# The wait for a scatter's landing in a mixture-of-experts kernel on one Trainium2 core: the copy of the scatter's targets is put ahead of it

## The chip, the cores and the metric

The kernel runs on one core of a Trainium2 chip. A core has four compute engines (TensorE, VectorE, ScalarE, GpSimd), a queue engine SyncE (SP) that mostly issues DMAs, and 16 DMA engines. The metric is the device time of one execution in microseconds, the median of several runs. Each engine runs its own instruction stream in order; the streams meet only at semaphores.

## The reference, cut to what matters

The layer has two halves. The first is attention: adaLN modulation, one combined input projection, differential attention beside grouped-query attention, an output projection and a residual. The second is a mixture of experts over 1024 tokens of width 1024. It is the second that the change touches:

```
s = sigmoid(h @ w_router)                      # 64 experts
idx, w = group-limited top 8 of 64, normalised # for each token
routed[token] += w * ((silu(h @ w_eg[e]) * (h @ w_eu[e])) @ w_ed[e])   # for its 8 experts e
x = x + gate * rmsnorm(routed + shared_expert(h))
```

Every token goes to 8 of 64 experts, so there are 8192 pairs of token and expert. An expert has a gate and an up matrix of 1024 x 256 and a down matrix of 256 x 1024, all float32.

## The kernel before

The program runs phase after phase: `front`, `attention`, `output_and_router` (which also runs the shared expert and writes its result to `y_d` in device memory), `routing_tables`, `experts`, `final`. The change lies in `experts` (from L1610).

**Blocks.** The pairs are sorted by expert and cut into blocks of 128 slots; the last block of an expert is padded. In this data that makes 104 blocks; an expert has one or two of them, seldom more. `routing_tables` makes a table with the expert, the first slot and the weight-ring place of each block. For each block n: 128 token rows of `h2_d` are gathered by index, transposed, multiplied with the expert's gate and up weights, passed through silu, scaled, transposed, multiplied with the down weights, and the 128 result rows are added to their tokens' rows in `y_d` by a scatter that accumulates.

**Precision.** Products are made from a high and a low part of both factors, three matmuls for one. ScalarE makes the high parts (`w_gate_up_high` L1747, `w_down_high` L1771) and VectorE the low parts (`w_gate_up_low` L1802, `w_down_low` L1831), for every block again.

**Who does what, in one turn n.** The four loops are written by hand and run the same number of turns, with different parts of the pipeline in one turn:

- SyncE loads each expert's weights into a ring of 5 places, when the last block that used the place has passed TensorE's down product (semaphore `dn`).
- TensorE: gate and up product of block n+1, transposes of n+2 (L1865), down product of n (`ps_ye`, L1893), transpose of the activation of n+1.
- ScalarE: high part of the activation of n, `w_down_high` of n, `w_gate_up_high` of n+2, silu of n+1, transposed rows of n+2, and then the result of n out of PSUM into one of two buffers `e_y`, in two halves (L1782 and L1784). Ahead of the first half it waits on `scat` for 16n + 16, which is the landing of the scatter of n-2, since that one read the same buffer.
- VectorE: the low parts in the same order, and `e_weight` and the gate.
- GpSimd: gathers the rows of block n+4 (a copy of 128 indices, L1692, then the indirect DMA, L1695), loads the indices of n+6 (L1683), and then scatters the result of n (a copy of the 128 target rows, L1704, then the indirect DMA, L1709).

**The scatters are kept one behind another.** A token's rows appear in blocks of several experts, and each scatter reads, adds and writes rows of `y_d`. So scatter n is not issued before scatter n-1 has landed: GpSimd waits on `scat` for 16n + 32 (the count starts at 32, from two writes of zeros). The target rows of block n come out of a ring of 8 columns (`ir`) into one of two small buffers (`si`). `carry` is a semaphore that nobody waits for.

**Order of time.** ScalarE's result of block n+1 waits for the landing of scatter n-1, and so does GpSimd's turn n. In the trace the two stand beside each other.

Of the kernel before, what the change touches and what calls it, by code (L numbers as in the profile page):

```python
# [1609 lines left out]
def experts(b, a, ident, tab, wgu, wdn, s_w, s_slots, h2_d, y_d, slot_d):  # L1610
# [3 lines left out]
    nc = b.nc  # L1614
    NS = SPLIT // 2
    RING = 8
    with ExitStack() as ph:
# [14 lines left out]
        ir = b.sb(ph, "e_index_ring", [P, RING], U32)  # L1632
        zero = b.sb(ph, "e_zero", [P, D])
        gi = [b.sb(ph, f"e_gather_index{u}", [P, 1], U32) for u in range(2)]
        si = [b.sb(ph, f"e_target_index{u}", [P, 1], U32) for u in range(2)]
# [4 lines left out]
        S = {n: b.sem(ph, "e_" + n) for n in (  # L1640
            "xT", "xH", "xL", "wH", "wL", "wused", "gu", "silu", "act", "aTp", "aH", "dh", "dl",
            "dn", "y", "weight", "rows", "target", "scat", "landed", "carry", "zeroed")}
# [4 lines left out]
        def read(eng, c, at, hi):  # L1647
            return eng.value_load(tab[0:1, c, ds(at, 1)], min_val=0, max_val=hi)

        def blocks(eng, body):  # L1650

            turns = eng.value_load(tab[0:1, 3, E:E + 1], min_val=1, max_val=NBLK // 2)
            with eng.Fori(0, turns) as i:
                for u in range(2):
                    body(i, i * 2 + u, u)
            return turns

        @block.sync
        def _(sp):

            def landed(n):
                sp.wait_ge(s_w[n % WS], (n // WS + 1) * 48)
                sp.sem_inc(S["landed"], 1)

            landed(0)
            sp.wait_ge(s_gather[1], 16)
            for n in range(PRE, WS):
                load_expert(sp, a, wgu, wdn, s_w, n)
                landed(n - 1)
            for n in range(WS, E):  # L1670
                done = read(sp, 3, n - WS, NBLK)
                sp.wait_ge(S["dn"], done * 2 + 1)
                load_expert(sp, a, wgu, wdn, s_w, n)
                landed(n - 1)
            landed(E - 1)

        @block.gpsimd
        def _(pool):
            def index(n, u):

                row = read(pool, 1, n, E * SEQ)
                pool.sem_inc(S["carry"], 1)
                pool.dma_start(ir[:, ds(n & (RING - 1), 1)], slot_d[ds(row, P), :]).then_inc(s_index[u], 16)  # L1683

            def gather(n, turn, u, first=False):

                pool.wait_ge(s_index[u], turn * 16 + 16)
                if not first:
                    pool.wait_ge(S["xT"], n * 2 - 2)
                    pool.wait_ge(S["weight"], n - 1)  # L1690
                pool.sem_inc(S["carry"], 1)
                nc.gpsimd.tensor_copy(gi[u][:], ir[:, ds(n & (RING - 1), 1)]).then_inc(S["rows"], 1)  # L1692
                pool.wait_ge(S["rows"], n + 1)
                pool.sem_inc(S["carry"], 1)
                pool.indirect_dma_start(xg[u][:], None, h2_d, bass.IndirectOffsetOnAxis(ap=gi[u][:, 0:1], axis=0),  # L1695
                                        bounds_check=SEQ - 1, oob_is_err=False).then_inc(s_gather[u], 16)

            def body(i, n, u):
                gather(n + 4, i + 2, u)
                index(n + 6, u)  # L1700

                pool.wait_ge(S["scat"], n * 16 + 32)
                pool.sem_inc(S["carry"], 1)
                nc.gpsimd.tensor_copy(si[u][:], ir[:, ds(n & (RING - 1), 1)]).then_inc(S["target"], 1)  # L1704

                pool.wait_ge(S["y"], n * 2 + 4)
                pool.wait_ge(S["target"], n + 1)
                pool.sem_inc(S["carry"], 1)
                pool.indirect_dma_start(y_d, bass.IndirectOffsetOnAxis(ap=si[u][:, 0:1], axis=0), yb[u][:], None,  # L1709
                                        bounds_check=SEQ + P - 1, compute_op=ALU.add).then_inc(S["scat"], 16)  # L1710


            for u in range(2):
                pool.wait_ge(s_slots[u], NT // 2 * TOPK * 16)
            index(0, 0)
            index(1, 1)
            for what in (xg[0], xg[1], zero):
                nc.gpsimd.memset(what[:], 0.0).then_inc(S["zeroed"], 1)
            pool.wait_ge(S["zeroed"], 3)
            gather(0, 0, 0, True)  # L1720
            gather(1, 0, 1, True)
            for n in range(2, 6):
                if n >= 4:
                    pool.wait_ge(s_index[n % 2], n // 2 * 16)
                index(n, n % 2)
            for h in range(2):
                pool.dma_start(y_d[SEQ + h * HD:SEQ + (h + 1) * HD, :], zero[0:HD]).then_inc(S["scat"], 16)
            gather(2, 1, 0)
            gather(3, 1, 1)
            turns = blocks(pool, body)  # L1730

            for u in range(2):
                pool.wait_ge(s_gather[u], turns * 16 + 32)
                pool.wait_ge(s_index[u], turns * 16 + 48)
            pool.wait_ge(S["scat"], turns * 32 + 32)
# [237 lines left out]
def ds(start, size):  # L1973
    return bass.ds(start, size)
# [80 lines left out]
```

## Time and profile before

| | us |
|---|---|
| median of 3 runs (lowest, highest) | 2325.89 (2323.56, 2327.89) |
| profiled execution | 2333.98 |
| its span, first to last instruction | 2332.3 |
| TensorE busy | 2035.9 (87%) |
| VectorE busy | 1432.4 (61%) |
| ScalarE busy | 1278.9 (55%) |
| GpSimd busy | 869.0 (37%) |
| first and last start of a block's result copy (L1782) | 1227.3, 2264.8 |

The times of the runs are of executions without the profiler; the profile is of another execution. The span is divided into phases only by what the instructions are: the expert phase is from about 1190 to 2280 us. "Idle before" of a group of instructions is the time in which their engine did nothing just before them, with what ended the wait. Where a wait stands for several semaphores, the profile names the one that came last by its own record, which can be the wrong one.

### The profile page before, as it was taken

Reading aid. Unit: us, or ns where it says so; the run is one execution under the profiler, and the core shown is the slowest. Engines: PE = TensorE matmul, PEld = TensorE weight load, DVE = VectorE, ACT = ScalarE, POOL = GpSimd, SP = SyncE. Lnnn points to the kernel's source line nnn. Section 1 sums busy time; section 2 is a strip of 40 time slices with the busy share of each in tenths; the row PEclk is TensorE's granted clock in tenths of the full one; section 3 lists DMA queues with packets and bytes.
Section 4 is the critical chain, followed back from the end, with each engine's and each line's share of the span. In section 5 each row is a group of like instructions: output and inputs, shape, how many; then the busy total and the mean of one; then the engine's idle time right before and its main releaser. Section 6 shows DMA issues by size and latency. Waiting matters only on the chain. (4 is left out here: it accounts for less than half of the span.)

```text
span 2332.3 us, 35734 instructions
## 1 busy us (share of the span) xinstructions
PE 2035.9 (87%) x9400; PEld 1452.3 (62%) x9401; DVE 1432.4 (61%) x2085; ACT 1278.9 (55%) x2004; POOL 869.0 (37%) x876
## 2 busy tenths in 40 slices
PE   4999995889888887899839999999999999999980
PEld 2776673655555554666427777777766777777760
DVE  3751564663358433455537777777676777777773
ACT  2421122556666565222127777776766777777761
POOL 1010103631155110044434455555444545544561
PEclk8999997899999998999969999999999999999995
DMA  6464436411221111343289998789999888789736
GB/s 248 140 190 118 130 115 187 114 32 39 44 48 39 39 35 63 133 92 101 56 255 293 317 336 247 231 233 328 336 330 331 260 232 229 203 258 334 202 61 233
DMA packets 284779, 420.25 MB, mean 180 GB/s; under 512 B 27233, under 2 KB 213345, under 8 KB 284689
## 3 DMA queue, kind: packets, MB, share of 16 engines
q1 hardware_dynamic: 213314, 281.25, 35.2%
q0 software_dynamic: 60496, 116.37, 22.6%
q10 hardware_dynamic: 10896, 21.71, 3.0%
q8 instruction: 40, 0.66, 0.1%
q14 instruction: 33, 0.27, 0.0%
HBM read 352.51 MB, written 91.54 MB: 190 GB/s over the span
## 5 line engine op out<-in xcount | busy, mean ns | idle before, releaser
L1802 DVE TENSOR_TENSOR w_gate_up_low<-w_gate_up,w_gate_up_high 128x1024 fp32r<-128x1024 f32 x318 | 378.2, 1217 | 15.9 <-ACT w_gate_up_high L1747 15.9
L1831 DVE TENSOR_TENSOR w_down_low<-w_down,w_down_high 128x2048 fp32r<-128x2048 f32 x104 | 238.4, 2292 | 161.5 <-ACT w_down_high L1771 161.5
L1747 ACT ACTIVATE w_gate_up_high<-w_gate_up 128x1024 fp32r x318 | 312.1, 1047 | 39.4 <-issue 28.6
L935 DVE TENSOR_REDUCE neg_max<-ps_scores 128x1 f32<-128x1280 f32 x128 | 190.3, 1490 | 223.6 <-PE ps_scores L1020 223.2
L1876 PE MATMUL ps_gu<-w_gate_up_high,gatheredT_high 128*128 128x512 f32 x630 | 256.1, 407 | 2.7 <-DVE gatheredT_low L1810 1.4
L1878 PE MATMUL ps_gu<-w_gate_up_high,gatheredT_low 128*128 128x512 f32 x630 | 248.7, 395 | 0.0
L1877 PE MATMUL ps_gu<-w_gate_up_low,gatheredT_high 128*128 128x512 f32 x630 | 248.6, 395 | 0.0
L1695 POOL DMA_INDIRECT gathered<-h_scratch,e_gather_index x108 | 195.6, 1811 | 96.5 <-POOL e_gather_index L1692 91.2
L1709 POOL DMA_INDIRECT y_scratch<-e_y,e_target_index x104 | 182.5, 1754 | 95.3 <-ACT e_y L1784 39.0
L1771 ACT ACTIVATE w_down_high<-w_down 128x2048 fp32r x104 | 199.6, 1919 | 29.2 <-issue 28.0
L1020 PE MATMUL ps_scores<-k_high_low,q_high 128*128 128x512 f32 (+1 forms) x384 | 167.5, 436 | 47.0 <-ACT probs L895 18.9
L1881 PE MATMUL ps_gu<-w_gate_up,gatheredT 128*128 x420 | 197.1, 591 | 0.0
L902 ACT ACTIVATE probsT<-ps_scores 128x512 f32<-128x512 f32 x240 | 138.2, 596 | 90.8 <-PE ps_scores L1034 90.8
L1034 PE MATMUL ps_scores<-ident,probs 128*128 128x128 f32 x960 | 146.3, 282 | 37.2 <-ACT probsT L902 34.2
L895 ACT ACTIVATE probs<-ps_scores,neg_max 128x1280 f32<-128x1280 f32 x96 | 127.5, 1328 | 80.6 <-DVE neg_max L935 80.4
L1034 PEld LDWEIGHTS ps_scores<-ident,probs 128*128 128x128 f32 x960 | 107.2, 143 | 100.7 <-ACT probsT L902 80.2
L1893 PE MATMUL ps_ye<-w_down_high,e_actT_high 128*128 128x512 f32 x416 | 139.1, 415 | 27.6 <-DVE w_down_low L1831 27.3
L1782 ACT ACTIVATE e_y<-ps_ye 128x512 f32<-128x512 f32 x104 | 62.4, 600 | 179.3 <-DMA y_scratch<-e_y,e_target_index 157.0
L1704 POOL COPY e_target_index<-e_index_ring 128x1 uint32 x104 | 53.1, 511 | 274.4 <-DMA y_scratch<-e_y,e_target_index 273.8
L654 PE MATMUL ps_chunk<-w_in_high,hT_high 128*128 128x512 f32 (+1 forms) x368 | 144.5, 393 | 7.8 <-DVE hT_low L495 6.1
L1865 PEld LDWEIGHTS ps_x<-ident,gathered 128*128 128x128 f32 x848 | 99.7, 141 | 79.1 <-issue 55.5
L1020 PEld LDWEIGHTS ps_scores<-k_high_low,q_high 128*128 128x128 f32 x384 | 75.2, 196 | 108.0 <-issue 74.5
(257 smaller groups left out, 4328.9 us busy)
## 6 DMA issues: line engine op xcount, KB each, us to landing
w_gate_up<-in_w_exp_gate SPq DMA_DIRECT2D x64, 1024.0 KB, 10.4
w_gate_up<-in_w_exp_up SPq DMA_DIRECT2D x64, 1024.0 KB, 13.9
w_down<-in_w_exp_down SPq DMA_DIRECT2D x64, 1024.0 KB, 15.5
w_mod_later<-in_w_mod ACTq DMA_DIRECT2D x32, 512.0 KB, 3.8
w_mod_first<-in_w_mod SPq DMA_DIRECT2D x4, 2048.0 KB, 15.6
w_in_raw<-in_w_in SPq DMA_DIRECT2D x32, 256.0 KB, 3.9
k_high_low<-k_scratch POOLq DMA_DIRECT2D x10, 640.0 KB, 8.0
values<-in_tokens SPq DMA_DIRECT2D x10, 512.0 KB, 11.3
```

The lines of the kernel that those rows point to most:

```text
L935: nc.vector.tensor_reduce(nm[:, n % 4:n % 4 + 1], S[:, span(u, r)], AX.X, ALU.max, negate=True).then_inc(s_m, 1)
L1020: last = nc.tensor.matmul(S[:, base + at:base + at + w], part[:, u % 2, cols], k2[:, kv_head(u, r), at:at + w], start=(part is qh), stop=( ...
L1034: last = nc.tensor.transpose(pT(u, kt)[:, j * P:(j + 1) * P], pr[:, u % 2, j, kt * P:(kt + 1) * P], ident[:])
L1695: pool.indirect_dma_start(xg[u][:], None, h2_d, bass.IndirectOffsetOnAxis(ap=gi[u][:, 0:1], axis=0), bounds_check=SEQ - 1, oob_is_err=Fals ...
L1747: act.activation(wH[:, 2 * j:2 * j + 2], wgu[:, ds(slot, 1), 2 * j:2 * j + 2].rearrange("p o k n -> p (o k) n"), ACT.Copy).then_inc(S["wH" ...
L1771: act.activation(dh[:], wdn[:, ds(slot, 1)].rearrange("p o k n -> p (o k) n"), ACT.Copy).then_inc(S["dh"], 1)
L1802: nc.vector.tensor_tensor(wL[:, 2 * j:2 * j + 2], wgu[:, ds(slot, 1), 2 * j:2 * j + 2].rearrange("p o k n -> p (o k) n"), wH[:, 2 * j:2 * ...
L1831: nc.vector.tensor_tensor(dl[:], wdn[:, ds(slot, 1)].rearrange("p o k n -> p (o k) n"), dh[:].bitcast(F32), ALU.subtract).then_inc(S["dl"], 1)
L1876: nc.tensor.matmul(psG[:], xH[:, k], wH[:, k], start=(k == 0), stop=False)
L1877: nc.tensor.matmul(psG[:], xH[:, k], wL[:, k], start=False, stop=False)
L1878: last = nc.tensor.matmul(psG[:], xL[:, k], wH[:, k], start=False, stop=(k == KD - 1))
L1881: last = nc.tensor.matmul(psG[:], xN[:, k - SPLIT], wgu[:, ds(slot, 1), k].rearrange("p o n -> p (o n)"), start=False, stop=(k == KD - 1))
```

## The change

In GpSimd's turn, the copy of the target rows is put ahead of the wait for the landing of the scatter in front. The waits for that copy and for the result `y` come next, and the wait for the landing is now the last thing ahead of the scatter. One increment of `carry` goes away.

```diff
                 gather(n + 4, i + 2, u)
                 index(n + 6, u)
 
+                nc.gpsimd.tensor_copy(si[u][:], ir[:, ds(n & (RING - 1), 1)]).then_inc(S["target"], 1)
+                pool.wait_ge(S["target"], n + 1)
+                pool.wait_ge(S["y"], n * 2 + 4)
                 pool.wait_ge(S["scat"], n * 16 + 32)
-                pool.sem_inc(S["carry"], 1)
-                nc.gpsimd.tensor_copy(si[u][:], ir[:, ds(n & (RING - 1), 1)]).then_inc(S["target"], 1)
-
-                pool.wait_ge(S["y"], n * 2 + 4)
-                pool.wait_ge(S["target"], n + 1)
                 pool.sem_inc(S["carry"], 1)
                 pool.indirect_dma_start(y_d, bass.IndirectOffsetOnAxis(ap=si[u][:, 0:1], axis=0), yb[u][:], None,
                                         bounds_check=SEQ + P - 1, compute_op=ALU.add).then_inc(S["scat"], 16)
```

## Rows read from the trace of the kernel before

**Rows 1.** The page: its first line, and the busy time of the engines.
```profile
span 2332.3 us, 35734 instructions
...
PE 2035.9 (87%) x9400; PEld 1452.3 (62%) x9401; DVE 1432.4 (61%) x2085; ACT 1278.9 (55%) x2004; POOL 869.0 (37%) x876
```

**Rows 2.** Line L1782: duration ns min/median/max, first and last start; all, then 1240 to 1300.
```profile
L1782 ACT ACTIVATE e_y<-ps_ye x104: 597/600/603, 1227.3 to 2264.8; 128x512 f32<-128x512 f32 x104
...
L1782 ACT ACTIVATE e_y<-ps_ye x6: 600/602/602, 1246.7 to 1295.2; 128x512 f32<-128x512 f32 x6
```

**Rows 3.** Waits from 1225 to 2280: waiter <- releaser: us in total, times, longest.
```profile
POOL e_target_index L1704 <- DMA y_scratch<-e_y,e_target_index: 273.8, 97, 5.8
DVE w_down_low L1831 <- ACT w_down_high L1771: 161.5, 103, 2.8
ACT e_y L1782 <- DMA y_scratch<-e_y,e_target_index: 157.0, 55, 4.9
...
PE ps_ye L1893 <- DVE w_down_low L1831: 27.3, 29, 1.8
```

**Rows 4.** Timeline of GpSimd: start us, us, instruction [idle before <- releaser].
```profile
1698.38 1.62 POOL L1709 DMA_INDIRECT y_scratch<-e_y,e_target_index  x1 [0.90 <-ACT e_y L1784]
...
1703.63 0.62 POOL L1683 DMA_DIRECT2D e_index_ring<-slot_scratch  x1
1708.21 0.18 POOL L1704 COPY e_target_index<-e_index_ring 128x1 uint32 x1 [3.96 <-DMA y_scratch<-e_y,e_target_index]
1709.31 1.63 POOL L1709 DMA_INDIRECT y_scratch<-e_y,e_target_index  x1 [0.92 <-ACT e_y L1784]
```

**Rows 5.** Line L1709 from 1697 to 1699: the one scatter's time to landing.
```profile
DMA to landing us min/median/max: 9.5/9.5/9.5
```

**Rows 6.** Timeline of ScalarE in the same stretch.
```profile
1697.11 0.60 ACT L1782 ACTIVATE e_y<-ps_ye 128x512 f32<-128x512 f32 x1 [3.35 <-DMA y_scratch<-e_y,e_target_index]
...
1708.02 0.60 ACT L1782 ACTIVATE e_y<-ps_ye 128x512 f32<-128x512 f32 x1 [3.61 <-DMA y_scratch<-e_y,e_target_index]
```

**Rows 7.** Line L1709 in 1590:1835, 1305:1425, 2085:2145, 1835:2085; landings where they stand.
```profile
L1709 POOL DMA_INDIRECT y_scratch<-e_y,e_target_index x23: 1617/1626/1634, 1592.0 to 1828.8; - x23
...
DMA to landing us min/median/max: 6.3/9.2/10.5
...
L1709 POOL DMA_INDIRECT y_scratch<-e_y,e_target_index x12: 1616/1625/2258, 1308.4 to 1421.6; - x12
...
L1709 POOL DMA_INDIRECT y_scratch<-e_y,e_target_index x6: 1621/1634/2160, 2087.1 to 2140.7; - x6
...
DMA to landing us min/median/max: 8.7/9.3/9.8
...
DMA to landing us min/median/max: 6.0/6.5/11.5
```

**Rows 8.** GpSimd's groups, 1590 to 1835: busy us, mean ns | idle before <- releasers.
```profile
L1709 POOL DMA_INDIRECT y_scratch<-e_y,e_target_index x23 | 37.4, 1626 | 21.9 <-ACT e_y L1784 19.1 <-issue 1.9 <-POOL e_target_index L1704 0.9
...
L1704 POOL COPY e_target_index<-e_index_ring 128x1 uint32 x23 | 6.3, 275 | 82.9 <-DMA y_scratch<-e_y,e_target_index 82.9
```

**Rows 9.** Timeline about 1147: an indirect DMA that VectorE's copy releases.
```profile
1147.49 0.17 DVE L1384 CAST slot_rows<-router_small 128x8 uint32<-128x8 f32 x1
...
1148.46 0.97 POOL L1092 DMA_INDIRECT slot_scratch<-token_numbers,slot_rows  x1 [5.25 <-DVE slot_rows L1384]
```

**Rows 10.** Windows: busy us by engine, then granted clock, DMA share, GB/s.
```profile
1590.00:1835.00 245.00, 226.97 (x1004) 169.00 (x1003) 173.98 (x205) 168.77 (x253) 122.06 (x115) 1.00 1.04 331
...
2085.00:2145.00 60.00, 59.61 (x274) 45.24 (x272) 45.69 (x55) 45.78 (x67) 27.26 (x29) 1.00 1.07 355
```

**Rows 11.** Timelines of GpSimd and VectorE about 2231.
```profile
2231.70 2.22 POOL L1704 COPY e_target_index<-e_index_ring 128x1 uint32 x1 [0.95 <-DMA y_scratch<-e_y,e_target_index]
...
2231.59 2.29 DVE L1831 TENSOR_TENSOR w_down_low<-w_down,w_down_high 128x2048 fp32r<-128x2048 f32 x1 [2.11 <-ACT w_down_high L1771]
```

**Rows 12.** Waits of the DMA queue of SyncE from 1590 to 1835.
```profile
SPq L1515 <- PE ps_ye L1893: 65.2, 12, 9.4
```

## The prediction

> **What bounds the kernel now.** The profiled execution took 2333.98 us, of which 2332.3 are the span; the other 1.7 lie around it [rows 1]. The median of the three runs shown is 2325.89, 8.1 below. I work in the profiled execution and subtract the 8.1 at the end. A difference under about 0.2%, 4.7 us, can't be told from no change here.
>
> The page has TensorE busy 87% of the span, so I first ask whether the scatter of a block can reach it. The changed lines run in the expert phase only, once per block of 128 slots. ScalarE's first copy of a block's result (L1782) starts 104 times from 1227.3 to 2264.8 [rows 2]: 1037.5 us over 103 periods, 10.07 each. At the start of the phase, where nothing waits for a scatter, six such starts go from 1246.7 to 1295.2: 9.70 each [rows 2], TensorE's own pace. So 1037.5 - 103 x 9.70 = 38.4 us are lost to something else, which caps what any edit of the scatter can bring.
>
> The waits say what it is [rows 3]. GpSimd's copy L1704 waited 273.8 us, 97 times, for a scatter to land; ScalarE's L1782 waited 157.0 us, 55 times, for the same landings; and at the end of the chain TensorE stood 27.3 us (29 times) before the down product for `w_down_low`, which itself waited for ScalarE. ScalarE is one block ahead of GpSimd: to overwrite `e_y` for block n+1 it needs the scatter of n-1, and GpSimd needs the same landing to go on with block n. So a late scatter holds ScalarE, then `w_down_high`, VectorE's `w_down_low` and TensorE. The 11 us between 27.3 and 38.4 I find in no single row; I count them to the same stalls, since without a stall the period is 9.70.
>
> The GpSimd timeline shows the loop closed [rows 4]. Scatter issued 1698.38, landing 9.5 later [rows 5], at 1707.9; e_y at 1708.02, that is 0.1 after the landing [rows 6]; GpSimd's copy at 1708.21, 0.29 after it, for 0.18; then 0.92 of idle time, and the next scatter at 1709.31. GpSimd had been free since 1704.25 (end of the index load). The two halves of e_y that this scatter moves were written a block earlier (L1782 at 1697.11 [rows 6]), so the product is not what it waits for, although the profile names L1784 as the releaser of the last 0.92.
>
> In the stretch 1590 to 1835 this loop is the bound: 23 scatters from 1592.0 to 1828.8 [rows 7], 10.76 each, 1.06 over TensorE's pace. Its parts: 0.29 from landing to copy, 0.275 mean copy, 0.95 mean idle before the scatter (21.9/23) [rows 8], and 10.76 - 0.29 - 0.275 - 0.95 = 9.24 from issue to landing (the median printed is 9.2).
>
> **What the change does, in order.** It adds no instruction and removes one semaphore increment (named `carry`, GpSimd's own). It moves one copy ahead of one wait; the waits for `y` and `target` too now come ahead of it.
>
> *The copy ahead of the wait.* It can start once the index load of the same turn is issued, at 1704.25 (1703.63 + 0.62), 3.7 us before the landing [rows 4]. No DMA is moved: gather and index load stay in front of it, the scatter behind it, and the next gather behind the scatter. In the dense stretch it is thus hidden by the landing even if it takes 2.2 us, as at 2231.70 [rows 11]. On the path this takes away 0.275 of copy and the 0.29 in front of it.
>
> *The wait that is now last.* Landing to start of the scatter is not in the trace of before. Bounds: below, zero, if the issue were made ready ahead (the index load starts at 1703.63 with no idle time before it [rows 4], so a DMA queued behind another one follows at once); above, 0.1 (what ScalarE needs after the same landing) plus the 0.92 that the issue takes behind a copy, 1.0. The nearest row is an indirect DMA that another engine's semaphore releases: VectorE's slot copy ends at 1147.66, the DMA starts at 1148.46, 0.80 [rows 9]. With the 0.1 of the landing I take 0.9. A loss is excluded here, since the old path held this same issue behind the copy.
>
> *The waits for `y` and `target`.* Nothing new: e_y of the block is finished some 11 us before its scatter (1697.11 and its second half 0.5 later, against 1709.31), and the copy's own completion lies before the landing. In the old order they came after the landing as well, at no cost.
>
> *Sum per block in the dense stretch.* Removed 0.29 + 0.275 + 0.95 = 1.515; added 0.9; saved 0.61. One of the 23 idle stretches was 1.9 and not 0.9, which may come again, so I count 0.57. New loop 10.76 - 0.57 = 10.19, still above 9.70.
>
> *What landings do when the loop is faster.* Weight loads share the 16 DMA engines, whose busy share is 1.04 at 331 GB/s there [rows 10]. At 10.19 a block it would be 331 x 10.76/10.19 = 350 GB/s. There is a row for such traffic: 2085 to 2145 ran at 355 GB/s, TensorE at 59.6 of 60, and its landings had a median of 9.3 [rows 7, 10]. So I add 0.1: 10.3. Bounds: nothing, and 1.3 (the longest landing of the stretch, 10.5, for the median 9.2).
>
> The Trainium skill, "DMA: Bandwidth & Descriptors", Latency and other measured facts, has the latency of HBM at 0.2 us on average and 2 us under high load. By it landings should lengthen well beyond 0.1, as an estimate by up to 1.8; the two stretches at 331 and 355 GB/s do not show that. Rival (c) is what it would be here.
>
> *Sum over the phase.* What stays lost: 22 periods of the dense stretch x (10.3 - 9.70) = 13. The earlier dense stretch, 12 scatters from 1308.4 to 1421.6, has 10.29 a block [rows 7], which less 0.57 is at TensorE's pace: nothing left. 2085 to 2145 has 10.7 a block, would have 10.2 and enters with slack: 2 left. Elsewhere landings are shorter: from 1835 to 2085 the median is 6.5, which with 1.5 is a loop of 8.0, and TensorE's pace already holds [rows 7]. Gain 38.4 - 15 = 23.4, say 24. Profiled execution 2310; on the median 2325.9 - 24 = 2302.
>
> *The copy in its new place.* In old order the copy came when VectorE was mostly waiting for the same landing. At the end of the phase it did not: copy at 2231.70 for 2.22 us, while `w_down_low` ran on VectorE from 2231.59 for 2.29 [rows 11]. Now it meets VectorE's work by chance. Where the landing is 3.7 us off it is hidden. Where landings are short (median 6.5 from 1835 to 2085 [rows 7]), GpSimd comes free about 0.7 before them (idle 0.95 less 0.29 [rows 11]); from scatter to scatter that is 5.87 (1698.38 to 1704.25) + 0.1 + up to 2.2 + 0.9 = 9.1, under 9.70, which costs nothing alone.
>
> The Trainium skill, "SBUF — State Buffer", Who interferes with whom, says that a VectorE instruction with two SBUF inputs and a GpSimd instruction reading SBUF exclude each other for the whole instruction, whichever came first. The row with 2.22 us agrees. By the same rule VectorE could be held by the moved copy, 0.18 at a time; 104 times that is 19 us if VectorE were last each time. VectorE itself waited 161.5 us before `w_down_low` [rows 3], so I count nothing.
>
> **The rivals.**
> (a) *All of it goes.* The issue after the landing costs 0.3 or less, or landings spread out: loop under 9.70 everywhere, gain 38.4, 2288. For: a queued DMA follows at once in rows 4. Against: 0.80 in rows 9.
> (b) *Landings eat it.* The DMA engines are full now; landings grow by 0.4 to 0.6 and the dense loop stays near 10.7. Each 0.1 costs 3.3 us over the 33 blocks of the two dense stretches, so 0.3 to 0.5 beyond the 0.1 counted leave a gain of 7 to 14: 2316. For: busy share 1.04. Against: the row at 355 GB/s.
> (c) *Slower.* The same place, past its break-even: with landings longer by over 0.8 (0.1 counted, and 24/33 = 0.7 more) the phase is longer than before. At the upper bound, 1.3, it is 0.5 x 33 = 16 us slower: 2342. Against: SP waits for a free weight slot, 65.2 us in this stretch [rows 12], so loads are paced by TensorE and don't pile up.
> (d) *The copy meets VectorE.* Short landings alternate with long ones (10.5): then 10.5 + 0.9 and 9.1 make 10.25 a block where before 10.5 + 1.4 and 6.3 + 1.4 made 9.85. Over some 20 such blocks 8 us are given back: gain 16, 2310. For: rows 11. Against: VectorE's two-input instructions run only part of the time, so 2.2 each time is the worst case.
> (e) *It does nothing*, if the last wait were for something else: 2326. Against: e_y 0.1 after the landing and the copy 0.19 behind it, block after block.
>
> **How the numbers follow.** Forecast 2302: 0.50; (a) 0.12; (b) 0.16; (c) 0.05; (d) 0.13; (e) 0.04. The range reaches from nearly (a) to (b): 2289 to 2319. Faster than 2321.2: forecast, (a), (d) and most of (b), 0.87; within: the rest of (b) and (e), 0.08; slower: (c), 0.05.
>
> **What would show it.** After: L1704 starts right behind L1683, with no wait for the scatter in front; L1709 waits for it instead, and starts 0.9 after the landing, which is 0.8 after ScalarE's e_y where that too waits for it; scatter to scatter in the dense stretch 10.2 to 10.3; TensorE's wait before L1893 falls from 27.3 to 10 or less. Wrong if landings there have a median over 9.6 (b, c), if L1709 starts over 1.1 after the landing, or if L1704 is long in blocks with short landings and TensorE waits there (d).

## The result, and the profile after

| | before | after |
|---|---|---|
| median (lowest, highest), us | 2326.89 (2323.56, 2330.24), 4 runs | 2307.07 (2301.09, 2309.87), 4 runs |
| ratio to before, 95% interval | | 0.9915 [0.9895, 0.9935] |
| profiled execution, its span | 2333.98, 2332.3 | 2306.8, 2305.2 |
| expert phase, first to last result copy | 1037.5 | 1017.7 |
| the same, over TensorE's pace (103 x 9.70 = 999.1) | 38.4 | 18.6 |

The change is faster by 19.8 us, 0.85%; the interval leaves out 1. All lines behind the edit are two lower now: the target copy is L1702, the scatter L1707, ScalarE's result copy L1780, TensorE's down product L1891. The page's first lines and L1780 (duration ns, first and last start) answer to [rows 1, 2]:

```profile
span 2305.2 us, 35630 instructions
...
PE 2027.0 (88%) x9400; PEld 1448.8 (63%) x9401; DVE 1432.9 (62%) x2085; ACT 1288.7 (56%) x2004; POOL 865.5 (38%) x876
...
L1780 ACT ACTIVATE e_y<-ps_ye x104: 597/600/618, 1222.3 to 2240.0; 128x512 f32<-128x512 f32 x104
```

The spans differ by 27.1, more than the medians. 19.8 of it is the phase (1037.5 less 1017.7). 5.0 lies ahead of the phase (first L1782 at 1227.3, first L1780 at 1222.3), where nothing was changed; over the fourteen profiled executions of this case that start falls anywhere from 1217 to 1228, so I take it for chance. 2.3 lies behind the phase.

The waits from 1225 to 2270 answer to [rows 3] (waiter <- releaser: us, times, longest):

```profile
DVE w_down_low L1829 <- ACT w_down_high L1769: 166.7, 101, 2.9
POOL y_scratch L1707 <- DMA y_scratch<-e_y,e_target_index: 157.8, 49, 5.9
POOL y_scratch L1707 <- ACT e_y L1780: 90.3, 26, 5.4
...
ACT e_y L1780 <- DMA y_scratch<-e_y,e_target_index: 61.8, 24, 4.0
...
ACT w_gate_up_high L1745 <- SPq L1663: 14.5, 3, 6.7
...
PE ps_ye L1891 <- DVE w_down_low L1829: 4.4, 8, 0.9
```

The copy no longer waits for a landing; the scatter does. ScalarE's wait for landings fell from 157.0 to 61.8, and TensorE's wait before the down product from 27.3 to 4.4. A line is new: ScalarE waited 14.5 us, three times, for SP's signal that an expert's weights had landed.

GpSimd's timeline (start us, us, instruction [idle before <- releaser]) answers to [rows 4]; behind it ScalarE's instruction that waited for the same landing [rows 6], and the landing of the scatter in front, issued at 1688.42 [rows 5]:

```profile
1694.22 0.61 POOL L1683 DMA_DIRECT2D e_index_ring<-slot_scratch  x1
1694.79 0.24 POOL L1702 COPY e_target_index<-e_index_ring 128x1 uint32 x1
1698.90 1.62 POOL L1707 DMA_INDIRECT y_scratch<-e_y,e_target_index  x1 [3.87 <-ACT e_y L1780]
...
1698.12 0.60 ACT L1780 ACTIVATE e_y<-ps_ye 128x512 f32<-128x512 f32 x1 [3.12 <-DMA y_scratch<-e_y,e_target_index]
...
DMA to landing us min/median/max: 9.6/9.6/9.6
```

The copy starts right behind the index load. The scatter in front lands at 1698.0 (1688.42 + 9.6), e_y starts 0.1 later, and the next scatter 0.78 after e_y, so 0.9 after the landing. The profile names `e_y L1780` as releaser, but that instruction is the next block's and merely waited for the same landing. Before, landing to scatter was 1.39.

The dense stretch, now from 1585 to 1802: the scatters, and the windows (us, busy us of PE, PEld, DVE, ACT and POOL with counts, granted clock, DMA share, GB/s), answering to [rows 7, 10]:

```profile
L1707 POOL DMA_INDIRECT y_scratch<-e_y,e_target_index x22: 1618/1630/2338, 1584.2 to 1801.1; - x22
...
DMA to landing us min/median/max: 8.5/9.1/11.2
...
1585.00:1802.00 217.00, 207.89 (x917) 156.20 (x916) 158.58 (x187) 157.01 (x230) 113.14 (x106) 0.98 1.05 329
2080.00:2140.00 60.00, 60.00 (x271) 45.31 (x270) 47.49 (x56) 47.22 (x68) 31.06 (x30) 1.00 1.03 330
```

Landings are as long as before (9.1, was 9.2), but the traffic did not rise: 329 GB/s, was 331 (the second row, where a rate of 355 had stood before, has 330). In ScalarE's timeline the new stall shows three times, 3.93 + 6.67 + 3.91 = 14.5 us:

```profile
1714.71 2.95 ACT L1745 ACTIVATE w_gate_up_high<-w_gate_up 128x1024 fp32r x3 [3.93 <-SPq L1663]
...
1728.69 2.96 ACT L1745 ACTIVATE w_gate_up_high<-w_gate_up 128x1024 fp32r x3 [6.67 <-SPq L1663]
...
1739.91 2.96 ACT L1745 ACTIVATE w_gate_up_high<-w_gate_up 128x1024 fp32r x3 [3.91 <-SPq L1663]
```

What the stalls cost is seen on TensorE: the starts of its down product, and windows of its granted clock:

```profile
1713.49 0.71 PE L1891 MATMUL ps_ye<-w_down_high,e_actT_high 128*128 128x512 f32 x2
...
1728.70 0.72 PE L1891 MATMUL ps_ye<-w_down_high,e_actT_high 128*128 128x512 f32 x2
...
1742.60 0.71 PE L1891 MATMUL ps_ye<-w_down_high,e_actT_high 128*128 128x512 f32 x2
...
1721.30:1724.20 2.90, 2.90 (x8) 2.27 (x7) 2.90 (x3) 0.72 (x1) 2.54 (x3) 0.50 1.10 335
1725.00:1732.00 7.00, 6.73 (x30) 4.59 (x28) 1.23 (x1) 3.31 (x5) 1.62 (x1) 1.00 1.04 357
```

The two periods of the down product are 15.2 and 13.9 us, 9.7 over twice 9.70. On ScalarE's result copies, by which the 18.6 is measured, the same stalls show as three periods of 11.3, 14.0 and 11.5, together 7.6 over the pace, since these copies were a little late already. So the stalls are some 40 to 50% of the 18.6. Not all of it is waiting: after TensorE had stood idle for 2.1 and 1.4 us, a matmul or two apart, its granted clock was 0.50, the lower level of 1.2 GHz, from 1721.3 to 1724.2, and its matmuls took 0.63 us where they take 0.40 at full clock; in the next stall it was 0.50 again from 1735.0 to 1737.9. As an estimate, 2.9 us at half the clock cost 1.4 us, so some 3 of the 9.7 us are the clock.

### The profile page after: what moved, and what is told of

Same layout as the page of the kernel before. It is cut to its first block and busy times, and to the rows that moved or that the text cites. A ratio compares the mean times of both kernels' runs of the same rounds, so it can differ in the third digit from the quotient of the medians.

```text
span 2305.2 us, 35630 instructions
## 1 busy us (share of the span) xinstructions
PE 2027.0 (88%) x9400; PEld 1448.8 (63%) x9401; DVE 1432.9 (62%) x2085; ACT 1288.7 (56%) x2004; POOL 865.5 (38%) x876
## 5 line engine op out<-in xcount | busy, mean ns | idle before, releaser
L1829 DVE TENSOR_TENSOR w_down_low<-w_down,w_down_high 128x2048 fp32r<-128x2048 f32 x104 | 238.5, 2293 | 166.7 <-ACT w_down_high L1769 166.7
L1707 POOL DMA_INDIRECT y_scratch<-e_y,e_target_index x104 | 211.6, 2035 | 314.5 <-DMA y_scratch<-e_y,e_target_index 157.8
L1695 POOL DMA_INDIRECT gathered<-h_scratch,e_gather_index x108 | 188.7, 1748 | 96.5 <-POOL e_gather_index L1692 91.2
L1891 PE MATMUL ps_ye<-w_down_high,e_actT_high 128*128 128x512 f32 x416 | 138.4, 414 | 4.5 <-DVE w_down_low L1829 4.4
L1874 PEld LDWEIGHTS ps_gu<-w_gate_up_high,gatheredT_high 128*128 128x128 f32 x630 | 120.1, 191 | 30.5 <-issue 5.7
L654 PE MATMUL ps_chunk<-w_in_low,hT_high 128*128 128x512 f32 (+1 forms) x368 | 136.3, 370 | 0.0
## 6 DMA issues: line engine op xcount, KB each, us to landing
w_gate_up<-in_w_exp_gate SPq DMA_DIRECT2D x64, 1024.0 KB, 11.7
values<-in_tokens SPq DMA_DIRECT2D x10, 512.0 KB, 11.3
```

What stands on the lines that cost most here:

```text
L654: last = nc.tensor.matmul(psC[:, n % 4, 0:w], H[:, k, tok], W[:, m % WR, 0:w], start=(k + i == 0), stop=(k == KD - 1 and i == 2))
L1829: nc.vector.tensor_tensor(dl[:], wdn[:, ds(slot, 1)].rearrange("p o k n -> p (o k) n"), dh[:].bitcast(F32), ALU.subtract).then_inc(S["dl"], 1)
L1874: nc.tensor.matmul(psG[:], xH[:, k], wH[:, k], start=(k == 0), stop=False)
```

## The experiments

All ratios are to the kernel before, in runs on the same chip. "Over the pace" is always last less first start of ScalarE's first result copy, less 999.1, in the profiled execution; "landings" is the median from 1590 to 1835, where the view gives one. For the kernel before they are 38.4 and 9.2, for the changed one 18.6 and 9.1. There is one profiled execution of each kernel, and in e3, e7, e8, e10 and e12 it was the fastest of its runs (e8's took 2323.36, against a median of 2329.92), so the last two columns are no measure of the median run there. The diffs are cut to the lines that matter; "..." marks what is left out.

| kernel | median us | ratio [95%] | over the pace | landings |
|---|---|---|---|---|
| e1_old_wait_order | 2305.53 | 0.9907 [0.9876, 0.9938] | 19.1 | 9.3 |
| e2_second_copy | 2326.47 | 0.9998 [0.9981, 1.0015] | 35.6 | 9.2 |
| e3_no_down_loads_old | 2295.65 | 0.9869 [0.9838, 0.9899] | 5.4 | |
| e4_no_down_loads_new | 2286.89 | 0.983 [0.9798, 0.9863] | 0.2 | 8.7 |
| e5_two_sums | 2307.93 | 0.9913 [0.9889, 0.9937] | 16.7 | 9.3 |
| e6_four_result_buffers | 2305.72 | 0.9898 [0.9873, 0.9923] | 17.0 | 9.3 |
| e7_ring_of_four | 2333.7 | 1.0027 [1.0013, 1.0042] | 47.3 | |
| e8_long_weight_rows | 2329.92 | 1.0012 [1.0, 1.0023] | 39.5 | 10.2 |
| e9_long_rows_two_sums | 2297.78 | 0.9876 [0.984, 0.9913] | 4.7 | 10.9 |
| e10_weight_rows_2k | 2303.51 | 0.9911 [0.9878, 0.9945] | 12.4 | 9.1 |
| e11_early_release | 2295.36 | 0.9855 [0.9827, 0.9882] | 11.3 | 9.1 |
| e12_early_2k_four_buffers | 2299.76 | 0.9878 [0.9854, 0.9902] | 6.8 | 9.1 |

**e1: the copy ahead, the other waits in the old order** (against the changed kernel).

```diff
                 nc.gpsimd.tensor_copy(si[u][:], ir[:, ds(n & (RING - 1), 1)]).then_inc(S["target"], 1)
-                pool.wait_ge(S["target"], n + 1)
-                pool.wait_ge(S["y"], n * 2 + 4)
                 pool.wait_ge(S["scat"], n * 16 + 32)
                 pool.sem_inc(S["carry"], 1)
+                pool.wait_ge(S["y"], n * 2 + 4)
+                pool.wait_ge(S["target"], n + 1)
+                pool.sem_inc(S["carry"], 1)
```

> The copy stays ahead of the landing wait, but the waits for the copy's completion and for the result y, and the second increment of carry, are put behind it, as they were before. Theory (the gain is the copy and its wake-up taken off the loop landing -> scatter -> landing): the scatter still starts 0.9 to 1.0 us after the landing, and the time stays at 2307, within 4. Rival (the order of the three waits did it, not the place of the copy): the scatter starts 1.2 us or more after the landing and the time goes back above 2318.

Its time is the changed kernel's within the intervals. ScalarE's and GpSimd's instruction behind one landing:

```profile
1645.59 0.60 ACT L1781 ACTIVATE e_y<-ps_ye 128x512 f32<-128x512 f32 x1 [3.11 <-DMA y_scratch<-e_y,e_target_index]
...
1646.63 1.63 POOL L1708 DMA_INDIRECT y_scratch<-e_y,e_target_index  x1 [4.10 <-ACT e_y L1781]
```

From e_y to the scatter 1.04, against 0.78 after the change and 1.29 before (1708.02 to 1709.31 [rows 4, 6]). So of the 0.5 taken out of this path the copy makes one half, and the other half is two waits, already satisfied, and an increment behind the landing. The trace is clear on 0.25 us; the time of the kernel can't resolve it. With the 0.1 to e_y the scatter starts 1.14 after the landing, between the 0.9 to 1.0 that I expected and the 1.2 of the rival. In this execution ScalarE waited 93.1 us for landings and only 4.1 for weights, against 61.8 and 14.5 in the changed kernel's, and yet as much is lost (19.1, 18.6): how the loss is shared between the two limits differs from one execution to the next.

**e2: a second copy behind the landing** (into a spare buffer, waited for), everything else as changed.

```diff
                 pool.wait_ge(S["scat"], n * 16 + 32)
                 pool.sem_inc(S["carry"], 1)
+                nc.gpsimd.tensor_copy(spare[u][:], ir[:, ds(n & (RING - 1), 1)]).then_inc(S["target"], 1)
+                pool.wait_ge(S["target"], n * 2 + 2)
+                pool.sem_inc(S["carry"], 1)
...
```

> The changed kernel with a second, useless copy of the same 128 targets put between the landing and the scatter. Theory: the loop gets back its old length (about 0.29 to the copy, 0.18 to 0.28 of copy, 0.9 to the issue), so the time is that of the kernel before, 2323 to 2330, and the scatters between 1590 and 1835 us are about 10.75 us apart. Rival (GpSimd's order in the turn matters, or the gain lay in other phases): it stays below 2315.

```profile
1661.80 0.60 ACT L1784 ACTIVATE e_y<-ps_ye 128x512 f32<-128x512 f32 x1 [3.21 <-DMA y_scratch<-e_y,e_target_index]
...
1661.85 0.18 POOL L1708 COPY e_spare_index<-e_index_ring 128x1 uint32 x1 [1.03 <-DMA y_scratch<-e_y,e_target_index]
1662.95 1.62 POOL L1711 DMA_INDIRECT y_scratch<-e_y,e_target_index  x1 [0.92 <-POOL e_spare_index L1708]
...
ACT e_y L1784 <- DMA y_scratch<-e_y,e_target_index: 177.3, 63, 4.4
PE ps_ye L1895 <- DVE w_down_low L1833: 23.4, 31, 1.9
```

A copy and a wait in the path again give all of it back: 2326.47, and TensorE's wait is 23.4 again (the scatters are 10.5 us apart from 1590 to 1835, a little under the 10.75 expected). That the gain comes from what stands between landing and scatter is shown.

**e3 and e4: the kernel before and the changed one without the loads of the down weights** from the sixth expert on (old down weights are used again), a third of the weight bytes less.

```diff
-    eng.dma_start(wdn[:, u], a["w_exp_down"][0, n].rearrange("(k p) n -> p k n", p=P)).then_inc(s, 16)
+    if n < WS:
+        eng.dma_start(wdn[:, u], a["w_exp_down"][0, n].rearrange("(k p) n -> p k n", p=P)).then_inc(s, 16)
...
```

> The kernel before, without the loads of the down weights after the first five experts (the products use stale down weights), so that the weight traffic falls by a third. Theory: landings of the scatters get shorter (median under 7.5 us in the stretch of single-block experts), the loop is under TensorE's 9.70 us a block everywhere, TensorE never waits for a scatter, and the time falls to 2286 to 2294 with the copy in its old place. Rival (landings do not depend on the weight traffic, or the loss of 38 us is not from them): it stays above 2310.

> The changed kernel with the same loads left out. Theory: 2286 to 2294 again, within 3 us of the other kernel without these loads, since there is no loop left to shorten; and TensorE never waits for weights. Rival (the change gains 20 us by something other than the loop): it is 15 to 20 us faster than the other kernel without these loads.

Windows of e3 and of e4, and e4's result copy:

```profile
1575.00:1815.00 240.00, 239.84 (x1083) 181.82 (x1082) 185.89 (x221) 187.28 (x272) 132.07 (x123) 1.00 0.92 261
```
```profile
1575.00:1815.00 240.00, 240.00 (x1089) 182.62 (x1088) 188.41 (x223) 191.55 (x273) 122.46 (x125) 1.00 0.92 262
...
L1781 ACT ACTIVATE e_y<-ps_ye x104: 600/601/608, 1222.0 to 2221.3; 128x512 f32<-128x512 f32 x104
```

With the traffic at 262 GB/s the whole of the loss is gone in e4: 999.3 us for 103 periods is TensorE's pace. So both limits, the chain of scatters and the weights, cost time only because of that traffic. The margin is small: I had expected landings under 7.5, and in e4 they still have a median of 8.7 in the dense stretch, which with 0.9 makes a loop of 9.6, just under 9.70. I had also expected 2286 to 2294 for both, and e3's 2295.65 is a little over it. I had expected e3 and e4 within 3 us of each other; they are 8.8 apart, with 5.4 and 0.2 over the pace, though ScalarE waited for no landing in either. What those 5 us of e3 are is not settled.

**e5: two accumulators in turn**, so that no scatter waits for the one in front, but for the one two back. The second accumulator is not added to the result.

```diff
+                pool.wait_ge(s_scat[u], i * 16 + 16)
...
-                pool.wait_ge(S["scat"], n * 16 + 32)
...
-                pool.indirect_dma_start(y_d, bass.IndirectOffsetOnAxis(ap=si[u][:, 0:1], axis=0), yb[u][:], None,
+                pool.indirect_dma_start((y_d, y2_d)[u], bass.IndirectOffsetOnAxis(ap=si[u][:, 0:1], axis=0), yb[u][:], None,
...
```

> The changed kernel with two accumulators in device memory: scatters of even blocks go to one, those of odd blocks to the other, each waits only for the scatter two blocks ahead, and the second accumulator is not added to the output (4.7 MB of zeros for it are written in an earlier, quiet phase). Theory (two limits: the chain of landings, and behind it the supply of weights at some 330 GB/s): no wait of TensorE for a scatter is left, but ScalarE still runs out of weights in the dense stretch, whose blocks stay at 10.1 us or more each; time 2294 to 2305. Rival (the chain of landings is the only bound): dense stretch at 9.70 and time 2285 to 2290.

```profile
ACT w_gate_up_high L1750 <- SPq L1666: 19.7, 5, 5.8
...
1590.00:1835.00 245.00, 234.27 (x1041) 176.94 (x1040) 180.21 (x215) 180.67 (x261) 111.16 (x118) 0.98 1.04 327
```

No result copy waited for a landing any more, yet the time is 2307.93, a few us above my range: the weights run out instead, 19.7 us, at 327 GB/s. The rival, by which the rest is the chain and the time falls to 2285 to 2290, falls.

**e6: four result buffers in place of two**, so that ScalarE need not wait for landings.

```diff
-        yb = [b.sb(ph, f"e_y{u}", [P, D]) for u in range(2)]
+        yb = [b.sb(ph, f"e_y{v}", [P, D]) for v in range(4)]
...
-                pool.wait_ge(S["scat"], n * 16 + 32)
+                pool.wait_ge(S["scat"], n * 16 + 64)
...
```

> The changed kernel with four e_y buffers in place of two (the turn unrolled for four blocks), so that ScalarE waits for the landing four blocks back; the scatters stay one behind another. Theory: the lag of the chain, at most about 11 us over the dense stretch, no longer reaches ScalarE, but the weights run out all the same: 2294 to 2306, with the waits of ScalarE on weights longer than the 14.5 us seen with two buffers. Rival (only the chain): 2285 to 2290.

```profile
ACT w_gate_up_high L1745 <- SPq L1663: 14.1, 5, 4.6
ACT w_gate_up_high L1745 <- PE ps_gu L1876: 6.3, 5, 4.4
```

The same picture as e5 by other means: no wait of ScalarE for landings, 14.1 us of waiting for weights (not more than the 14.5 of the changed kernel, as I had expected), 2305.72. Taking the chain away alone brings nothing that the runs resolve.

**e7: a weight ring of four places.**

```diff
-WS = 5
+WS = 4
```

> The changed kernel with a weight ring of 4 places in place of 5. Theory: the stalls between 1715 and 1742 us in the changed kernel are the ring running dry after some 14 single-block experts in a row; with one place less (3.1 MB, some 10 us of supply) it runs dry earlier and loses about 10 us more: 2313 to 2323. Rival (those stalls are an accident of that execution, such as one slow load): 2304 to 2310.

```profile
ACT w_gate_up_high L1745 <- SPq L1663: 65.8, 19, 5.8
...
ACT e_y L1780 <- DMA y_scratch<-e_y,e_target_index: 11.4, 5, 3.4
```

Waits for weights go from 14.5 to 65.8 and the waits for landings nearly vanish; 2333.7, 26.6 us over the changed kernel, where I expected 6 to 16. The direction is as said; I had not counted that the other two dense stretches would run dry too: 14.7 us of the 65.8 are waited before 1430, 37.3 from 1550 to 1850, and 13.7 after 2050.

**e8 and e10: longer pieces for the gate and up weights**, 8 KB and 2 KB for 1 KB, the same bytes in the same order of experts (8 KB first, then one line of the 2 KB form).

```diff
-    eng.dma_start(wgu[:, u, :, 0:FE], a["w_exp_gate"][0, n].rearrange("(p k) n -> p k n", k=KD)).then_inc(s, 16)
-    eng.dma_start(wgu[:, u, :, FE:], a["w_exp_up"][0, n].rearrange("(p k) n -> p k n", k=KD)).then_inc(s, 16)
+    eng.dma_start(wgu[:, u, 0], a["w_exp_gate"][0, n].rearrange("(p k) n -> p k n", k=KD)).then_inc(s, 16)
+    eng.dma_start(wgu[:, u, 1], a["w_exp_up"][0, n].rearrange("(p k) n -> p k n", k=KD)).then_inc(s, 16)
...
+    eng.dma_start(wgu[:, u, :, 0].rearrange("p j k n -> p j (k n)"), a["w_exp_gate"][0, n].rearrange("(p j k) n -> p j (k n)", j=KD // 2, k=2)).then_inc(s, 16)
...
```

> The changed kernel with gate and up weights kept apart in each ring place, so that a partition's 8 KB of each lie in one piece in device memory and in SBUF (1 KB pieces before). Theory: the same bytes take less DMA time (a 4 KB packet moved 24 bytes a ns here, a 1 KB packet 21), so weights arrive 5% sooner, the ring doesn't run dry, and landings are a little shorter: 2290 to 2301. Rival (supply is not a limit, or the piece size does not matter): 2304 to 2310.

> The changed kernel with gate and up weights in 2 KB pieces (two rows of k together), between the 1 KB of the changed kernel and the 8 KB that made landings 1.1 us longer. Theory (longer pieces speed up the weights and hold up the scatter's own packets behind them, in proportion): landings in the dense stretch of 9.3 to 9.6 us, hardly any wait of ScalarE for weights, and a time of 2303 to 2313, the gain in supply spent on the chain. Rival (only pieces over 4 KB hold up the scatter): landings as in the changed kernel, no waits for weights, 2296 to 2302.

e8, its DMA summary and the scatters from 1590 to 1835, and its waits:

```profile
DMA packets 17638, 77.08 MB, mean 315 GB/s; under 512 B 3548, under 2 KB 3548, under 8 KB 13027
...
L1707 POOL DMA_INDIRECT y_scratch<-e_y,e_target_index x24: 1612/1626/2569, 1588.9 to 1833.6; - x24
...
DMA to landing us min/median/max: 6.2/10.2/12.1
...
ACT e_y L1781 <- DMA y_scratch<-e_y,e_target_index: 124.7, 38, 5.3
...
PE ps_ye L1893 <- DVE w_down_low L1831: 27.7, 27, 2.2
```

e8 is a clear miss: I expected 2290 to 2301, it took 2329.92. ScalarE never waits for weights in the dense stretch, with a third of the packets (17638, was 53151 before the change). But the landings of the scatters have a median of 10.2, and the chain is the bound again, 10.64 us a block (244.7/23); TensorE's wait is back at 27.7. With 2 KB pieces (e10) landings stay at 9.1, where I expected 9.3 to 9.6 and the rival had them unchanged; only 0.4 us are waited for weights, and the time is 2303.51, within the interval of the changed kernel. Its five runs reach from 2298.16 to 2316.73, too wide to choose between the 2303 to 2313 expected and the rival's 2296 to 2302.

**e9: e8's 8 KB pieces with e5's two accumulators** (the second again not added), both edits as above.

```diff
+    eng.dma_start(wgu[:, u, 0], a["w_exp_gate"][0, n].rearrange("(p k) n -> p k n", k=KD)).then_inc(s, 16)
...
+                pool.indirect_dma_start((y_d, y2_d)[u], bass.IndirectOffsetOnAxis(ap=si[u][:, 0:1], axis=0), yb[u][:], None,
```

> The changed kernel with both the long weight rows (8 KB pieces) and the two accumulators (second one not added to the output), that is with both limits named so far lifted at once. Theory (chain of landings and supply of weights are the two limits, and each covers the other: one alone gives nothing): weights don't run out, nothing waits for the scatter in front, TensorE keeps 9.70 a block within 6 us over the phase, time 2286 to 2295. Rival (a third thing bounds the dense stretch, such as the DMA engines altogether): it stays at 2303 or more.

```profile
1575.00:1815.00 240.00, 236.75 (x1071) 179.88 (x1071) 185.05 (x219) 187.75 (x267) 117.92 (x123) 1.00 1.02 344
...
ACT w_gate_up_high L1750 <- SPq L1666: 10.7, 6, 4.1
```

2297.78, a little above the 2286 to 2295 expected: with the chain gone the long pieces bring 344 GB/s, the most of any kernel in this stretch, and still 10.7 us of waiting for weights. It separates the two effects of e8: more bytes per second, and longer landings for the scatters beside them (10.9 here, where nothing waits for the scatter in front).

**e11: each load waits only for what it overwrites.** SP waited for the last down product (`dn`) before all three loads of an expert. Now the gate and up loads wait for the gate and up product alone (`gu`), a block earlier, and only the down load waits for `dn`. The DMAs stay the same and in the same order.

```diff
-                sp.wait_ge(S["dn"], done * 2 + 1)
-                load_expert(sp, a, wgu, wdn, s_w, n)
+                load_expert(sp, a, wgu, wdn, s_w, n, (S["gu"], done), (S["dn"], done * 2 + 1))
...
```

> The changed kernel with the gate and up part of a ring place loaded again as soon as the last gate and up product has used it, about a block's time ahead of the down product that frees the place now; the down weights wait as before. Theory (the ring of five runs dry in the dense stretch, and a ring of four lost 26 us more): two thirds of a load come up to 9.7 us sooner, worth more than half a place, so ScalarE's waits for weights in the dense stretch fall from 14.5 us to under 5, and the time to 2296 to 2303. Rival (the DMA engines are full and the rate alone counts, not the lead): 2304 to 2310.

```profile
L1783 ACT ACTIVATE e_y<-ps_ye x104: 597/600/603, 1218.5 to 2228.9; 128x512 f32<-128x512 f32 x104
...
1575.00:1815.00 240.00, 233.96 (x1047) 175.86 (x1046) 182.26 (x216) 173.62 (x263) 136.64 (x119) 1.00 1.06 336
...
ACT e_y L1783 <- DMA y_scratch<-e_y,e_target_index: 96.9, 41, 4.1
PE ps_ye L1894 <- DVE w_down_low L1832: 6.4, 12, 1.2
```

2295.36 (2293.28 to 2297.17), 11.7 under the changed kernel's median (by the two ratios to the kernel before it would be 14): the lowest median of the kernels that compute the whole layer. No wait for weights is left. What remains over the pace, 11.3, I put down to the chain, since ScalarE's waits for landings are the only long ones left. It was not run on the wait order of before.

**e12: e11 with 2 KB pieces and four result buffers**, the edits of e11, e10 and e6 together.

```diff
+                load_expert(sp, a, wgu, wdn, s_w, n, (S["gu"], done), (S["dn"], done * 2 + 1))
...
+        yb = [b.sb(ph, f"e_y{v}", [P, D]) for v in range(4)]
...
+            wgu = b.sb(ex, "w_gate_up", [P, WS, KD // 2, 2, 2, FE])
```

> The changed kernel with the early release of the gate and up part, the 2 KB weight pieces and four e_y buffers together. Theory (after the early release only the chain of landings is left, 11 us over the phase, and two more e_y buffers let ScalarE run ahead of a chain that lags by no more than that): ScalarE waits neither for weights nor for a scatter by more than 5 us in all, the blocks keep 9.70 within 4 us over the phase, and the time is 2284 to 2291. Rival (with the chain no longer pacing the blocks the weights run out again, as they did with four buffers alone): 2293 to 2300.

2299.76 from six runs, and these spread from 2290.83 to 2307.07. The profiled execution is the fastest of them and shows neither limit (2.2 us of waits for landings, none for weights, 6.8 over the pace). I expected 2284 to 2291. What the slower executions did no profile shows, so this stays open. The time lies in the rival's range, 2293 to 2300, but its reason, weights that run out again, is not in the one profile. It is not better than e11.

## Why the prediction came out as it did

Predicted 2302 with a range of 2289 to 2319, measured 2307.07: a gain of 19.8 where 24 was forecast. By its steps:

- *The cap, 38.4 us from ScalarE's result copies.* Held: e4 came down to TensorE's pace and no lower (0.2 over it).
- *The copy ahead of the wait, hidden.* Held: L1702 follows L1683 at once. Rival (e) falls.
- *0.9 from landing to scatter.* Held: 0.90, taken from an unlike row, VectorE's 0.80 [rows 9], plus 0.1. Rival (a) needed 0.3 or less.
- *The waits for `y` and `target` "after the landing as well, at no cost".* Wrong: e1 has 0.25 us for them and the increment. This did no harm to the sum, since I had taken old and new path whole.
- *Landings in the faster loop, +0.1.* In the dense stretch better than forecast: 9.1 for 9.2. In the light stretch behind it, now from 1815 to 2065, the median rose from 6.5 to 8.2, which I had not foreseen; with 0.9 that is 9.1, still under 9.70, and costs nothing. Why it rose no run shows. Rivals (b) and (c), which both rest on longer landings, don't happen in the changed kernel. e8 shows that (c)'s mechanism exists: with 1.0 more the time is 2329.92.
- *Traffic rises from 331 to 350 GB/s.* This is the step that failed. I took one row of 60 us at 355 GB/s for proof that the rate could be had, and the full DMA share of 1.04 only as an argument about landings. In the changed kernel it is 329 GB/s at a share of 1.05, and across the kernels with all their loads the stretch of 240 us or so never had more than 344 (e9). SP's loads say the same (first two rows below): from 1640.9 to 1752.8 it issued ten experts' gate weights, 12.4 us apart, and waited for a free place only once, for 3.3 us; before the change ten took from 1642.0 to 1749.5, 11.9 apart, so the weights came no faster. Over the same 22 periods of blocks (36 to 58) the changed kernel moved 75.4 MB (330 GB/s for 228.6 us) and the kernel before 78.9 (333 for 237.0); the 3.5 MB between them, an estimate from these rows, are about one expert (3.1 MB), used out of the ring and not put back. A loop with nothing else in its way uses up the ring of five experts faster than that rate fills it, and then ScalarE waits for weights: 14.5 us. SP, which waited for free places 65.2 us before [rows 12], still waited 20.9 us in the same stretch (third row below), 15.1 of it ahead of the stalls, time in which the next weights could have been fetched; e11, which lets it fetch earlier, removes ScalarE's wait and 11.7 us of the time.
- *Dense loop 10.3.* Measured 10.39 between the result copies of blocks 36 and 58 (fourth row below) against 10.77 before, but not for my reason. The stalls for weights, a term that my sum did not have, carry 7.6 of its loss. 10.3 was nearly right by two errors of opposite sign, which is luck: the chain alone is 10.0 to 10.2 (9.1 + 0.9 by the medians; 10.16 in e10 over the same blocks, where next to no weights are waited for, fifth row), and the weights add the rest, with the lower clock of TensorE behind the stalls, which I had not foreseen either.
- *Left lost 15.* Measured 18.6, of it 15.2 in the 24 periods of the dense stretch (13 forecast), 3.4 elsewhere (2 forecast). The rest of the gap between 24 and 19.8 is below what the runs resolve.
- *Rival (d), the copy meets VectorE.* Partly there. The copy's mean fell from 511 to 395 ns, so it meets VectorE less than before. But the scatter's own issue now does (last rows below): a mean of 2035 ns was 1754 before, and the longest is 3623 ns, was 3261. All 38 issues of over 1.75 us start while a two-input instruction runs on VectorE (16 of 16 before); 26 of the 66 shorter ones do so too, so the meeting alone doesn't lengthen every one. In all it is 29 us more of GpSimd's time (211.6 against 182.5), mostly where it has slack; TensorE's waits do not show it. (A small slip in my sum: 10.5 + 1.4 and 6.3 + 1.4 make 9.8 a block, not 9.85, and the 8 us would be 9.)

SP's gate loads in the changed kernel and before; its wait in the changed kernel from 1590 to 1835; the result copies of blocks 36 to 58 in the changed kernel and in e10; and two of the changed kernel's groups:

```profile
L1515 SPq DMA_DIRECT2D w_gate_up<-in_w_exp_gate x10: 550/551/3332, 1640.9 to 1752.8; - x10
...
L1515 SPq DMA_DIRECT2D w_gate_up<-in_w_exp_gate x10: 550/551/2027, 1642.0 to 1749.5; - x10
...
SPq L1515 <- PE ps_ye L1891: 20.9, 6, 8.4
```
```profile
L1780 ACT ACTIVATE e_y<-ps_ye x23: 598/600/615, 1573.9 to 1802.5; 128x512 f32<-128x512 f32 x23
...
L1781 ACT ACTIVATE e_y<-ps_ye x23: 597/600/602, 1571.2 to 1794.6; 128x512 f32<-128x512 f32 x23
```
```profile
L1702 POOL COPY e_target_index<-e_index_ring 128x1 uint32 x104 | 41.1, 395 | 0.0
...
L1707 POOL DMA_INDIRECT y_scratch<-e_y,e_target_index x104 | 211.6, 2035 | 314.5 <-DMA y_scratch<-e_y,e_target_index 157.8
```

The Trainium skill, "DMA: Bandwidth & Descriptors", Where 436 GB/s comes from, puts what HBM gives one core at about 358 GB/s. No stretch of 60 us or more that was read passes it (355 for 60 us [rows 10]; 357 for the 7 us from 1725 to 1732), but with all loads the kernels stay below it when the load lasts, at 315 (e8) to 344 (e9); with scatters that read and write beside the weights, the page's figure is no rate to plan with here. For the rule of the Trainium skill on HBM latency under load, which the prediction weighed, no run is a test: between 329 and 355 GB/s the landings stay at 9.1 to 9.3, but they are 6.5 at 220 GB/s and 9.2 at 331 in the kernel before, and nothing here parts the latency of HBM from the time in the queues.

So the mechanism was right. That the sum came so near is in part luck: the chain alone gave back more than forecast, and the weights, which the sum left out, took that and a little more. Nothing held them to that size; with a ring of four (e7) the same limit costs more than the change gains.

## What to carry to other kernels

Where a chain of transfers is the bound, put everything that doesn't need the landing ahead of the wait for it, the satisfied waits too: here 0.5 us a block, and 19.8 us in all. Then ask at once what the faster loop consumes: with a DMA share over 1.0 the next limit is the weights, and the rate of one short stretch doesn't show that more can be had for long. Loads that each wait only for the last reader of their own buffer (e11) gave 11.7 us more, with the same DMAs.

## What was not expected of the hardware

- Two satisfied semaphore waits and one increment between a landing and an indirect DMA cost 0.25 us on GpSimd (e1: 1.04 against 0.78).
- Long pieces on one queue lengthened another queue's transfers: 8 KB in place of 1 KB takes the scatters' landings from 9.1 to 10.2 us and eats all that the change had won; 2 KB does no such thing (9.1).
- When weights run out, the clock adds to the loss: behind TensorE's idle times in two of the stalls its granted clock was 0.50 for 2.9 us.
- A ring one place shorter costs 27 us (e7), far more than the one-fifth less buffer suggests, since it runs dry in every dense stretch.
- GpSimd's issue of one scatter, 1.63 us in the median, takes up to 3.6 us.
